# First eight projection tiles of each layer on the unnormalised x, with the inverse root applied as PSUM is emptied

## What is computed

```
h = rmsnorm(x, ln_mix[l])            # x * rsqrt(mean(x*x) + EPS) * gain
(hq, hf, hi, hg, rq, rk, rv, rg, sq, sk, sv, gate_logits) = jnp.split(h @ w_in[l], IN_SPLITS, axis=-1)
qb = rope(rq, positions, ret_inv_freq)   # ang = pos * inv_freq; cos(ang), sin(ang)
kb = rope(rk, positions, ret_inv_freq)
```

## Time and profile before

| | us |
|---|---|
| median of 3 runs (lowest to highest) | 2566.93 (2566.46 to 2568.69) |
| the profiled execution, its own time | 2566.51 |
| its span on the core | 2564.7 |
| PE busy in it | 2464.0 (96%) |
| DVE, ACT, POOL busy | 1679.2, 1310.8, 1148.5 |

### The profile page before, as it was taken

One profiled execution on the slowest core, in us unless ns is written; L12 is line 12 of the kernel. 1 busy time (PEld: TensorE's weight loads), 2 busy tenths in 40 slices (PEclk: granted clock), 3 DMA queues, 4 the chain that ended last, 5 costly groups with the idle time before them and its releaser, 6 DMA issues.

```text
span 2564.7 us, 49244 instructions
## 1 busy us (share of the span) xinstructions
PE 2464.0 (96%) x17162; PEld 2306.6 (90%) x17162; DVE 1679.2 (65%) x2976; ACT 1310.8 (51%) x2020; POOL 1148.5 (45%) x461
## 2 busy tenths in 40 slices
PE   7999999999999999999989999989999999999998
PEld 6999999899999898888879999989999999988887
DVE  8465721599988555777683656225999875567776
ACT  4475544455545444454545755444555454445544
POOL 4865775689666000000067667666986640000000
PEclk8999999999999999999989999999999999999999
DMA  5543453355656766777545334434556666667775
GB/s 194 170 135 124 156 175 126 135 164 180 247 207 246 230 204 221 243 238 239 189 165 174 132 124 156 165 131 132 172 191 236 223 238 224 208 222 241 242 242 167
DMA packets 187160, 487.94 MB, mean 190 GB/s; under 512 B 14465, under 2 KB 81025, under 8 KB 182401
## 3 DMA queue, kind: packets, MB, share of 16 engines
q1 hardware_dynamic: 180384, 444.83, 52.7%
q10 hardware_dynamic: 6624, 41.16, 4.0%
HBM read 451.34 MB, written 34.60 MB: 189 GB/s over the span
## 4 chain that ended last, share of the span: by engine, by line
PE 81%; DVE 8%; issue 4%; ACT 3%; POOL 2%; DMA 1%; DVEq 0%; ACTq 0%; POOLq 0%; SPq 0%
PE banks L785 27%; PE banks L446 15%; PE banks L448 15%; PE banks L447 15%; PE banks L761 2%; POOL w_lo L384 2%; PE banks L596 1%; DVE arena L1477 1%; ACT w_hi L816 1%; PE banks L709 1%; PE banks L680 1%; PE banks L661 1%; DMA gates_dram<-o_f 1%; DMA o_f<-gates_dram 0%; DVE arena L1412 0%
## 5 line engine op out<-in xcount | busy, mean ns | idle before, releaser
L384 POOL TENSOR_TENSOR w_lo<-ring,w_hi 128x1024 fp32r<-128x1024 f32 x457 | 1148.3, 2524 | 1404.0 <-ACT w_hi L816 1403.8
L816 ACT ACTIVATE w_hi<-ring 128x1024 fp32r<-128x1024 f32 x777 | 818.2, 1056 | 407.4 <-PE banks L785 331.6
L446 PE MATMUL banks<-h_r,w_hi 128*128 128x256 f32 x3408 | 980.3, 288 | 35.7 <-DVE h_r L1282 32.6
L447 PE MATMUL banks<-h_r,w_hi 128*128 128x256 f32 x3408 | 971.6, 285 | 0.0
L448 PE MATMUL banks<-h_r,w_lo 128*128 128x256 f32 x3408 | 971.4, 285 | 0.0
L446 PEld LDWEIGHTS banks<-h_r,w_hi 128*128 128x128 f32 x3408 | 660.0, 194 | 44.7 <-DVE h_r L1282 35.8
L447 PEld LDWEIGHTS banks<-h_r,w_hi 128*128 128x128 f32 x3408 | 661.1, 194 | 3.0 <-issue 0.5
L448 PEld LDWEIGHTS banks<-h_r,w_lo 128*128 128x128 f32 x3408 | 660.6, 194 | 0.0
L785 PE MATMUL banks<-w_hi,o_r 128*128 128x512 f32 x2048 | 560.6, 391 | 4.4 <-DVE o_r L1640 4.4
L785 PEld LDWEIGHTS banks<-w_hi,o_r 128*128 128x128 f32 x2048 | 381.4, 189 | 80.5 <-DVE o_r L1640 4.9
L1608 DVE TENSOR_TENSOR w_lo<-ring,w_hi 128x1024 fp32r<-128x1024 f32 x320 | 390.0, 1219 | 10.3 <-ACT w_hi L816 10.3
(11 more groups left out here) (246 smaller groups left out, 2486.5 us busy)
## 6 DMA issues: line engine op xcount, KB each, us to landing
ring<-in_stream SPq DMA_DIRECT2D x780, 512.0 KB, 3.3
gates_dram<-o_f ACTq DMA_DIRECT2D x32, 1024.0 KB, 6.1
o_f<-gates_dram SPq DMA_DIRECT2D x32, 1024.0 KB, 7.4
arena<-in_mem ACTq DMA_DIRECT2D x2, 1024.0 KB, 9.4
arena<-in_keys ACTq DMA_DIRECT2D x2, 1024.0 KB, 4.9
arena<-in_c_decay ACTq DMA_DIRECT2D x2, 768.0 KB, 4.6
x<-in_x SPq DMA_DIRECT2D x4, 256.0 KB, 4.3
out_dram<-arena SPq DMA_DIRECT2D x4, 256.0 KB, 2.6
```

The costliest lines, as they stand in the source:

```text
L384: pool.tensor_tensor(w_lo[:, s, :], ring[:, s, :], w_hi[:, s, :], ALU.subtract).then_inc(sem(f"low{s}"), 1)
L446: pe.matmul(out, lhs[0], rhs[0], start=first, stop=False)
L447: pe.matmul(out, lhs[0], rhs[1], start=False, stop=False)
L816: act.activation(w_hi[:, s, :], ring[:, s, :], ACT.Copy).then_inc(sem(f"high{s}"), 1)
```

## The change

- PE's first eight tiles multiply u = x * gain, split into `u_r[0]` and `u_r[1]` before any root is known; the sum of squares is made on PE between the first and the second tile. DVE copies each of the eight out of its bank and multiplies by rinv as it does (`first_evac`).
- DVE makes h for the later tiles, two chunks at a time, in PSUM banks 0 to 3, and the temporaries of the angles in banks 6 and 7, between these copies.
- The splits of slots 0 to 2 and the making of u stand at the end of the layer before (for layer 0 before the loop), DVE making those `w_lo`; slot 3 is in the next head. POOL begins at group 1.
- At the start, the DMA of slot 0's weights goes ahead of x.

```
 # start, SP
+            sp.dma_start(smalls[:, :, :], a["small"]).then_inc(sem("small_loaded"), 16)
+            load(0, 0)
+            for k in range(0, KC, 2):
+                sp.dma_start(x[:, k:k + 2, :], a["x"][:, k:k + 2, :]).then_inc(sem(f"x{k}_loaded"), 16)
+            load(0, 1)
...
 # head, PE
-                with pe.Fori(0, 2) as i:
-                    for s in range(SLOTS):
-                        feature_tile(G_RQ + i, s, T_RQ + i * SLOTS + s, hr, 0 if s == 0 else None)
+                for t in range(2 * SLOTS):
+                    feature_tile(G_RQ + t // SLOTS, t % SLOTS, T_RQ + t, u_r, parts=None if t else "u_ready")
+                    if t == 0:
+                        rms_pairs(l * SQUARES, 0)
+                        pe.wait_ge(sem("consts"), N_CONST)
+
+                ev("p_ready", SLOTS, SLOTS)
 # head, ACT
-                for k in range(KC):
-                    parts(h[:, k, :], hr[0][:, k, :], "h_made", k + 1, 3 * KC, "h_high")
-                    if k in (1, 4, 7):
-                        split_next(-1, (1, 4, 7).index(k) + 1)
+                split_next(-1, 3)
+                take_root(l * 3, 0)
+                for t in range(2 * SLOTS):
+                    split_next(G_RQ + t // SLOTS, t % SLOTS)
+                    if t < SLOTS:
+                        parts(pair_of(t), hr[0][:, 2 * t:2 * t + 2, :], "p_made", t + 1, SLOTS, "p_high")
...
 # end of a layer, ACT
+                split_next(GROUPS - 1, 0)
+                split_next(GROUPS - 1, 1)
                 act.activation(spare[:, :], eps[:, :], ACT.Sqrt)
...
+                split_next(GROUPS - 1, 2)
                 ev("down_half", NK, NK)
                 y_out(0, 0)
                 y_out(0, 1)
...
+                    unscaled_high(b, small)
+                    if b:
+                        squares(b - 1)
+                squares(KC // 2 - 1)
+
+            take_root(DEPTH * 3, 0)
 # DVE
+            def unscaled_low(k, gain, at):
+
+                dve.wait_ge(sem("u_high"), at + k + 1)
+                dve.scalar_tensor_tensor(u_r[1][:, k, :], x[:, k, :], gain[:, k:k + 1], u_r[0][:, k, :],
+                                         ALU.mult, ALU.subtract).then_inc(sem("u_ready"), 1)
...
+                def first_evac(t):
+
+                    used(dve, l * GROUPS + G_RQ + t // SLOTS, t % SLOTS)
+                    dve.tensor_tensor(part(0, 2 * HEADS, T)[:, t, :], tile_out(t), rinv[:, :], ALU.mult
+                                      ).then_inc(sem("bank_free"), 1)
...
+                first_evac(4)
+                pair_low(2)
+                ev("rope_tables", 32, 32)
+                link(dve.tensor_copy(posf, posi))
+                link(dve.tensor_scalar(ang, posf, freq[:, 0:1], None, ALU.mult))
+                first_evac(5)
+                pair_low(3)
+                angle(0, sinb, 0.0)
+                first_evac(6)
+                angle(0, cosb, 0.25)
+                first_evac(7)
+                link(dve.tensor_scalar(ang, posf, freq[:, 1:2], None, ALU.mult))
+                angle(1, sinb, 0.0)
+                angle(1, cosb, 0.25)
 # end of a layer, DVE
+                link(dve.tensor_copy(small[:, :], smalls[:, bass.ds(DEPTH - 1 - l, 1), :].rearrange("p a n -> p (a n)")))
+                for s in range(SLOTS - 1):
+                    low_whole(l * GROUPS + GROUPS, s)
```

More of the change, by code:

```diff
@@ L371, in _ @@
                 sp.dma_start(a["out"][:, k:k + 2, :], h[:, k:k + 2, :]).then_inc(sem("stored"), 16)
[L372 to L373 removed]
+            sp.wait_ge(sem("slot3_loaded"), (DEPTH * GROUPS + 1) * 16)
             sp.wait_ge(sem("stored"), KC // 2 * 16)
[L376 removed]
+        N_CONST = 4 * 16
         @block.gpsimd
@@ L820, in _, with squares, unscaled_high @@
             act.activation(spare[:, :], eps[:, :], ACT.Sqrt)
-            for k in range(0, KC, 2):
-                act.wait_ge(sem(f"x{k}_loaded"), 16)
-                act.activation(square[:, k:k + 2, :], x[:, k:k + 2, :], ACT.Square).then_inc(sem("squared"), 1)
+            def squares(b):
+                act.activation(square[:, 2 * b:2 * b + 2, :], x[:, 2 * b:2 * b + 2, :], ACT.Square
+                               ).then_inc(sem("squared"), 1)
+            def unscaled_high(b, gain):
+                for k in (2 * b, 2 * b + 1):
+                    act.activation(u_r[0][:, k, :], x[:, k, :], ACT.Copy, scale=gain[:, k:k + 1]).then_inc(sem("u_high"), 1)
+            high_part(0, 0)
+            act.wait_ge(sem("small_loaded"), 16)
+            for b in range(KC // 2):
+                act.wait_ge(sem(f"x{2 * b}_loaded"), 16)
+                unscaled_high(b, smalls[:, 0, 0:KC])
+                if b:
+                    squares(b - 1)
+            high_part(0, 1)
+            squares(KC // 2 - 1)
+            high_part(0, 2)
             act.sem_inc(sem("bank_free"), 2)
@@ L1241, in _, with low_whole, invert @@
                 link(dve.tensor_tensor(lower_all[:, d, :], lower_all[:, d, :], lbp[:, 0, :], ALU.subtract))
+            def low_whole(g, s):
+                dve.wait_ge(sem(f"high{s}"), g + 1)
+                dve.tensor_tensor(w_lo[:, s, :], ring[:, s, :], w_hi[:, s, :], ALU.subtract).then_inc(sem(f"low{s}"), 1)
+            def unscaled_low(k, gain, at):
+                dve.wait_ge(sem("u_high"), at + k + 1)
+                dve.scalar_tensor_tensor(u_r[1][:, k, :], x[:, k, :], gain[:, k:k + 1], u_r[0][:, k, :],
+                                         ALU.mult, ALU.subtract).then_inc(sem("u_ready"), 1)
+            low_whole(0, 0)
+            dve.wait_ge(sem("small_loaded"), 16)
+            dve.tensor_copy(small[:, :], smalls[:, 0, :])
+            for k in range(KC):
+                dve.wait_ge(sem(f"x{k // 2 * 2}_loaded"), 16)
+                unscaled_low(k, smalls[:, 0, 0:KC], 0)
+            low_whole(0, 1)
+            low_whole(0, 2)
             dve.wait_ge(sem("consts"), N_CONST)
             link(dve.tensor_copy(iota[:, :], iota_f[:, :]))
-            def scaled(n, gain, done, then=None):
+            def invert(n):
                 dve.wait_ge(sem("rooted"), n + 1)
@@ L1250, in scaled @@
                 dve.wait_ge(sem("inverted"), n + 1)
+            def scaled(n, gain, done, then=None):
+                invert(n)
                 for k in range(KC):
@@ L1691, in _, with add_y @@
                 dve.tensor_copy(y_rows[:, 1, 0:512], bank[:, 2, :]).then_inc(sem("y_out10"), 1)
-                for b in range(4):
+                def add_y(b):
                     ev("y_turned", b + 1, 4)
```

120 lines of the change are left out of this document (68 added, 52 removed).

## The result

| | before | after |
|---|---|---|
| median of 22 runs each, same chips (lowest to highest), us | 2568.57 (2565.42 to 2573.42) | 2572.22 (2568.03 to 2577.60) |
| ratio, 95% interval | | 1.0015 (1.0008 to 1.0022) |
| span of the profiled execution | 2564.7 | 2569.2 |

The change costs 3.7 us where 12 less were forecast. It is 0.15%, within the 0.2% that the prediction calls no change, and the interval lies wholly on the slow side. The forecast, its range and its sign are wrong.

What follows compares the result with a forecast made beforehand. PE bounds 81% of the chain, with DVE's angles the heads' second bound. Gains of 9.7 (layer 0) and 6.0 (layer 1) less 3.7 at the end make 12.0: 2566.9 to 2555.0 us, range 2549 to 2561.5.

Steps and rivals of the forecast that it cites:

- rivals b and c: DVE's queue: operations with a bank dearer, 2559, chance 0.06; or POOL holding DVE up after all, 2593, chance 0.06.
- DVE's queue from the inverse to tile 7's copy: Each layer's head: copies, products for h, lows and angle operations sum to 20.0 us, plus some 1.7 of waits.
- PE's wait at the rotation: Each layer's head: PE finishes its eight tiles about 3.8 us before DVE reaches tile 7's copy, and waits.
- the additions' delay at the border: Between the layers: the additions to x start 1.3 us later, at 1280.35 instead of 1279.05, behind the third split and w_lo.
- the end: Last layer: root 7.35 to 7.5 us after the first addition instead of 5.16; with the 1.3 delay, 3.7 later in all.
- PE on tile 0 from 8.3.: Layer 0's head: PE starts its first tile at 8.3 us, once the first parts of u are made.
- The second pair starts 9.6 after tile 7's copy.: Layer 0's head: rv's second pair starts 9.6 us after that copy, at 50.8, which is 9.7 earlier than before.
- The border: Between the layers: tile 0 at 1284.2, root 1293.2, second pair of rv 1326.7, which is 6.0 us earlier than before.
- rival (a): Border of the layers: PE back only at 1286.9, clock low, and a slow first sum: 2563; chance 0.17 for 2558 to 2563.
- From 60.47 and 1332.70 on, all engines stand to each other as they will after the change.: From rv's second pair on in both layers: how much earlier that pair starts was taken as the gain.
- The prediction's own sign of being wrong: The forecast is wrong if any head gains under 3 us, or a new wait appears behind rv's second pair.
- (d): The head's gain isn't passed on, the second pair waiting for weights or tables: near no change, chance 0.05.

Runs made afterwards that it cites:

- e1: The changed kernel with ACT's first credits (bank_free and the others) at the top of its list, ahead of slot 0's split: 2569.21 us, ratio 0.9998 to before.
- e6: The changed kernel with tile 7's copy ahead of the second angle and the sines between the copies of rv's two pairs: 2565.83 us, ratio 0.9985 to before.
- e5: The changed kernel with one short pause per layer in POOL's list, ahead of group 42's first w_lo: 2566.11 us, ratio 0.9983 to before.
- b4: The kernel before with a one-column write, waited for, ahead of the selection's second L1568 operation on DVE: 2575.02 us, ratio 1.0028 to before.
- e3: The changed kernel with tile 7's copy ahead of the second angle and the sines behind both of rv's pairs: 2578.20 us, ratio 1.0030 to before.
- e4: The changed kernel with slot 2's split behind ACT's squares and its w_lo behind DVE's low parts of u: 2571.29 us, ratio 1.0006 to before.
- b5: The kernel before with the two sines between the copies of rv's first and second pair: 2565.31 us, ratio 0.9985 to before.
- b3: The kernel before with a one-column write, not waited for, ahead of the selection's second L1568 operation on DVE: 2569.16 us, ratio 0.9993 to before.
- b2: The kernel before with a short pause in POOL's list behind every w_lo: 2574.80 us, ratio 1.0020 to before.

## Why the prediction was wrong

Right: that operations with a bank are not held up by POOL (rivals b and c out: the angle operations take 0.42 to 0.43 each, also those that took 0.29 in SBUF, and the products for h 0.48 in either memory; the 65 ns for a source in PSUM, an estimate from the table in the Trainium skill, "VectorE: DVE Perf Modes", section on the TRN2 errata, don't show between `tensor_tensor` in SBUF, 0.42, and with a bank, 0.42); DVE's queue from the inverse to tile 7's copy (21.1 from the inverse's end, of 21.7); PE's wait at the rotation (3.48, of 3.8); the additions' delay at the border (1.03, of 1.3); DVE's jump hidden; the end (7.68, of 7.35 to 7.5). What failed, in order of time:

1. **"PE on tile 0 from 8.3."** The data was in time, the credit of the banks was not: 12.48. I had costed the squares and splits on ACT and not what stands behind them in its list. 3.9 at the start, 3.0 to 4.4 at the end (e1).
2. **"The second pair starts 9.6 after tile 7's copy."** It took 11.5, and 11.2 in layer 1, and the sines did not set it. I had named the wait of 3.8 and left out that the clock falls behind it: the rotation runs at 0.50 from 45.8 to 49.3 (its four matmuls are 0.86 apart instead of 0.43), most of the 1.9. The angles, the bound before, were in time. e6 shows wait and fall to be real loss.
3. **The border.** PE came back 4.2 behind its last transpose, where the forecast had 3.8 behind the last release and rival (a) 5.9. Tile 0 ran at 0.50, the sum did not (3.61), and the root ended 0.9 behind the forecast's place. DVE's queue to tile 7's copy gave 0.9 back, and the rotation took its 1.6 (step 2). Layer 1's head so gives 4.4 of the forecast's 6.0 (2.50 earlier than before, from an entry that was 1.93 late).
4. **"From 60.47 and 1332.70 on, all engines stand to each other as they will after the change."** This is the step that turns the sign. They stood to each other as before to about 0.2 us: at the selection ACT's split is 3.2 ahead of its old time, POOL's w_lo and DVE 3.0. These 0.2 decide that POOL goes first: 2.3 of wait and 1.5 to 2.1 of lower clock per layer, 8.3 in all. e5 gives back 6 to 8, b4 takes 6.5 from the other kernel. Where the 0.2 comes from no run shows. It isn't the size of the head's gain: POOL goes first in e1, e3, e4 and e6 too, whose second pairs start up to 4.6 apart, and DVE in b5 as in before.

The sum again: -12.0, + 4 (credits), + 1.9 (fall behind the rotation, layer 0), + 1.6 (layer 1's head), + 8.3 (selection) = + 3.8; measured + 3.7 by the medians and + 4.5 between the two profiled executions, so the last unit agrees in part by luck. The prediction's own sign of being wrong, a new wait behind the second pair, is what came. Of my rivals (d), "the head's gain isn't passed on", is what happened. But I had it wait for weights or tables, gave it 0.05, and argued only against those two. I never looked at the place where DVE's chain, and not PE's own work, sets PE's next start, although 1.61 of wait at 623.43 and DVE's L1568 stood in the trace.

What stays open: by the medians the parts e4 and e6 are known to 1 or 2 us only; and the profiled executions differ by falls of the clock that come and go (only the change fell at 301.8 and 2110.9, 1.3 and 1.5 lost; only before at 1578.3, 1.3 lost; and the change lost another 1.5 between 722 and 735, where its wait is 6.0 against 5.5 and the low clock lasts longer behind it), which no run here separates from chance.

## What to carry to other kernels

A gain at the head of a long program is worth what it still is at the next place where another engine's chain sets PE's start: go there in the trace of before, and for each contest of DVE and POOL for SBUF read what releases either side and by how little it is won. A shift of both sides by 2 to 4 us changed nothing here; 0.2 us of one against the other turned it. When work is moved onto an engine, read its list to the end for credits and presets that others need first. Behind a wait, price the granted clock too, and mend waits in pairs: taking one away (e3) can make a later one that costs more.

## What the hardware did that I had not expected

- At the end of a w_lo under 0.1 us decides whether DVE or POOL goes next, and the loser is held for the whole of the winner's operation. DVE starts 0.07 to 0.08 behind that end in all kernels without a pause but b4 (0.21). POOL starts 0.02 to 0.04 behind it where ACT's split has ended 0.14 to 0.16 ahead (the change, e1, e3, e4, e6), and 0.08 to 0.10 behind it where the split ends within 0.03 of it (before, b3, b4, b5). DVE takes 2.28 or 4.4 to 4.5, POOL 2.4 or 4.2 to 4.6, but for one w_lo of 3.9 in b2, in 14 profiled executions and both layers.
- An operation reported as started may be waiting: L1653's 4.51 begins at 609.99, 0.04 behind the w_lo that holds it.
- The granted clock at a wait of PE, in the same 14 executions, the idle start left out and only where it was at 1.00 before: it fell to 0.50 at each of 100 waits of 3.4 us or more and at two of 3.0, and stayed at 1.00 at all 44 of 1.41 to 1.80. Of 48 waits of 1.83 to 2.64 it fell at 34, and at one wait that all kernels share, of 2.68 to 2.71, in 20 cases of 28. So the change could lose by one more wait of 3.9 what it saved in three short ones.
- Where PE jumps back over the layer's loop it was idle for 3.0 to 4.5 us in the change and its variants. The row's releaser names DVE's low parts of u, of which in the change the first was there 3.1 earlier (1283.75). That the jump fills this time is inferred, not seen in a row.
